# The high and low halves of the activations as one 512-column operand, in a split-precision transformer block on one core

## The reference, cut to what matters

```
for i in range(DEPTH):                                  # 2 layers
    sh1, sc1, g1, sh2, sc2, g2 = _ada(c, ada_w[i], ada_b[i])     # silu(c) @ ada_w + ada_b
    hx = _modulate(_rmsnorm(x, norm1_g[i]), sh1, sc1)
    yx = _mla(...)  if layer 0 else  _fourier_mix(hx, fno_w[j])  # both end in a 2048 x 2048 product
    x = x + g1 * yx
    x = x + g2 * _conv_ffn(_modulate(_rmsnorm(x, norm2_g[i]), sh2, sc2), ...)
return _rmsnorm(x, final_norm_g)

def _conv_ffn(h, w_up, conv_w, conv_b, w_down):         # D_FF = 5632
    u = _dwconv3(h @ w_up, conv_w, conv_b)              # 2048 -> 11264, then 3 taps along the tokens
    val, gate = jnp.split(u, 2, axis=-1)
    return (val * silu(gate)) @ w_down                  # 5632 -> 2048
```

## Time and profile before

| | |
|---|---|
| median of 3 runs | 2375.63 us (2371.57 to 2377.6) |
| the profiled execution's own time: first to last instruction | 2380.2 us |
| PE busy, its weight loads busy | 2240.8 us, 2151.0 us |
| DVE busy | 1778.1 us |
| ACT busy | 1116.4 us |
| the two square stages | about 535 to 632 and 1490 to 1588 us |
| up, layer 0: main part, second part | about 656 to 1021, 1223 to 1366 us |
| down, layer 0: main part, second part | about 1030 to 1213, 1366 to 1434 us |
| up, layer 1: main part (with ada steps to about 1800), second part | about 1610 to 1977, 2162 to 2300 us |
| down, layer 1: main part, second part | about 1977 to 2162, 2300 to 2366 us |

### The profile page before, as it was taken

How to read it: one execution, slowest core, us unless ns; L and a number is a source line. 1 busy time by engine, 2 the same in 40 slices (tenths; PEclk the granted TensorE clock), 3 DMA queues, 4 the chain that set the end, 5 groups by cost and what they waited for, 6 DMA issues and landing times.

```text
span 2380.2 us, 47926 instructions
## 1 busy us (share of the span) xinstructions
PE 2240.8 (94%) x17414; PEld 2151.0 (90%) x17414; DVE 1778.1 (75%) x2221; ACT 1116.4 (47%) x1441; POOL 178.9 (8%) x152
## 2 busy tenths in 40 slices
PE   5788888889899999999999999989999999999997
PEld 3268777779899999999999998989999999999997
DVE  4989677759888888878868886988886664445665
ACT  5742344433356666633335534336666663334542
POOL 0013100004300000000000040430000000000013
PEclk9989899989899999999989999989999999999999
DMA  8957434439677787779978781877775555555553
GB/s 304 339 184 278 153 133 141 129 104 328 237 259 271 271 273 276 271 279 371 370 257 272 278 261 49 304 261 257 273 247 184 186 183 170 185 185 180 183 184 124
DMA packets 149967, 546.90 MB, mean 230 GB/s; under 512 B 17040, under 2 KB 17552, under 8 KB 149648
## 3 DMA queue, kind: packets, MB, share of 16 engines
q1 hardware_dynamic: 149904, 546.04, 66.2%
HBM read 543.88 MB, written 2.10 MB: 229 GB/s over the span
## 4 chain that ended last, share of the span: by engine, by line
PE 81%; DVE 10%; issue 5%; ACT 2%; POOL 1%; DMA 1%; DVEq 0%; SPq 0%; ACTq 0%; POOLq 0%
PE bank L1133 24%; PE bank L1134 23%; PE bank L1135 23%; DVE w_lo L686 2%; PE bank L1163 2%; DVE acc L711 2%; PE bank L1139 1%; PE bank L1141 1%; PE bank L1140 1%; DVE w_lo L742 1%; PE bank L1316 1%; PE bank L1186 1%; PE bank L1195 1%; DMA x<-xT 1%; ACT w_hi L456 0%
## 5 line engine op out<-in xcount | busy, mean ns | idle before, releaser
L456 ACT CAST w_hi<-raw 128x1024 fp32r<-128x1024 f32 x638 | 665.3, 1048 | 644.1 <-PE bank L1135 596.9
L1133 PE MATMUL bank<-h_hi,w_hi 128*128 128x256 f32 x3216 | 920.3, 286 | 23.8 <-DVE w_lo L686 18.8
L686 DVE TENSOR_TENSOR w_lo<-raw,w_hi 128x1024 fp32r<-128x1024 f32 x642 | 780.7, 1228 | 187.9 <-ACT w_hi L456 187.8
L1134 PE MATMUL bank<-h_lo,w_hi 128*128 128x256 f32 x3216 | 917.3, 285 | 0.0
L1135 PE MATMUL bank<-h_hi,w_lo 128*128 128x256 f32 x3216 | 917.0, 285 | 0.0
L1133 PEld LDWEIGHTS bank<-h_hi,w_hi 128*128 128x128 f32 x3216 | 625.3, 194 | 28.2 <-issue 25.4
L1134 PEld LDWEIGHTS bank<-h_lo,w_hi 128*128 128x128 f32 x3216 | 625.4, 194 | 0.0
L1135 PEld LDWEIGHTS bank<-h_hi,w_lo 128*128 128x128 f32 x3216 | 624.9, 194 | 0.0
L711 DVE SCALAR_TENSOR_TENSOR acc<-ada,silu_c,acc 128x1024 f32<-128x1024 f32 x320 | 427.1, 1379 | 12.2 <-issue 9.4
L1133 PE MATMUL bank<-a_hi,w_hi 128*128 128x256 f32 x1408 | 395.9, 281 | 1.7 <-DVE a_lo L690 1.7
L1134 PE MATMUL bank<-a_lo,w_hi 128*128 128x256 f32 x1408 | 395.3, 281 | 0.0
(11 more groups left out here) (185 smaller groups left out, 2435.6 us busy)
## 6 DMA issues: line engine op xcount, KB each, us to landing
raw<-weights SPq DMA_DIRECT2D x642, 512.0 KB, 4.5
ada<-ada_late SPq DMA_DIRECT2D x320, 512.0 KB, 4.9
early<-ada_early SPq DMA_DIRECT2D x64, 512.0 KB, 5.4
ctx_s<-ctxT SPq DMA_DIRECT2D x1, 2048.0 KB, 7.8
x<-xT SPq DMA_DIRECT2D x1, 2048.0 KB, 12.2
outT<-h_pre SPq DMA_DIRECT2D x4, 512.0 KB, 2.7
dft_s<-dft SPq DMA_DIRECT2D x1, 768.0 KB, 5.6
conv_s<-conv SPq DMA_DIRECT2D x2, 176.0 KB, 3.7
```

The costliest lines, as they stand in the source:

```text
L456: act.copy(w_hi[:, slot, :], raw[:, slot, :]).then_inc(hi_done, 1)
L686: dve.tensor_tensor(w_lo[:, slot, :], raw[:, slot, :], w_hi[:, slot, :].bitcast(f32), ALU.subtract)\
L1133: pe.matmul(out, wh, hi_part, start=first, stop=False)
L1134: pe.matmul(out, wh, lo_part, start=False, stop=False)
```

## The change

The high and the low part of each activation tensor become one tensor with the part as second index (`h_hl`, `a_hl`, `f_hl`), so that one matmul can stream both: w_hi meets 512 columns (256 high, 256 low) and fills a whole bank, and w_lo then meets the 256 high columns and accumulates into the bank's first half. The bank's two halves have to be added afterwards. In `residual` a second multiply-add out of the second half follows the first, and waits for it. In the up stages ACT copies the second half into `part` and DVE adds the first half to it into `up_s`; this frees the bank. All three taps then read `up_s`, and the split that came after the taps comes between that addition and the taps. Silu now waits for `conv_done`, which the right tap raises.

```diff
-            mm = product(bank[4 + t][:, 0:SEQ], (c0 + e) % RING, k % 8, hh[:, k, :], hl[:, k, :], ...)
+            mm = halves(bank[4 + t], (c0 + e) % RING, k % 8, src[:, :, k, :], k == 0, k == KT - 1)
...
+            def halves(bank_, slot, u, pair, first, last):
+
+                cols = slice(u * UNIT, (u + 1) * UNIT)
+                pe.matmul(bank_[:, :], w_hi[:, slot, cols], pair, start=first, stop=False)
+                return pe.matmul(bank_[:, 0:SEQ], w_lo[:, slot, cols], pair[:, 0, :], start=False, stop=last)
...
 (ACT, in pair)
                     for g in range(2):
                         act.wait_ge(chunk_used, c + 2 * g + 2)
+                        act.copy(part[:, g, :], bank[(T0 + 2 * s + g) % 4][:, SEQ:2 * SEQ]).then_inc(part_done, 1)
+                        split(c + 6 + g, c0 + 2 + g)
                         taps = conv_s[:, bass.ds(2 * f + g, 1), :]
-                        act.activation(cv[:, s, g, :], bank[(T0 + 2 * s + g) % 4][:, 0:SEQ], ACT.Identity,
+                        act.wait_ge(tile_taken, T + g + 1)
+                        act.activation(cv[:, s, g, :], up_s[:, g, :], ACT.Identity,
                                        bias=taps[:, :, 3], scale=taps[:, :, 1]).then_inc(mid_done, 1)
-                        split(c + 6 + g, c0 + 2 + g)
-                    act.wait_ge(tile_taken, T + 2)
+                    act.wait_ge(conv_done, 2 * Pn + 2)
                     act.activation(cv[:, s, 1, :], cv[:, s, 1, :], ACT.Silu).then_inc(silu_done, 1)
...
 (DVE, residual)
-                dve.scalar_tensor_tensor(xm, bank[4 + e][:, 0:SEQ], g, xm, ALU.mult, ALU.add).then_inc(y_free, 1)
+                dve.scalar_tensor_tensor(xm, bank[4 + e][:, 0:SEQ], g, xm, ALU.mult, ALU.add).then_inc(y_half, 1)
+                dve.wait_ge(y_half, n_half)
+                dve.scalar_tensor_tensor(xm, bank[4 + e][:, SEQ:2 * SEQ], g, xm, ALU.mult, ALU.add).then_inc(y_free, 1)
...
 (DVE, in pair)
+                        dve.wait_ge(part_done, 2 * Pn + g + 1)
+                        dve.tensor_tensor(u, b[:, 0:SEQ], part[:, g, :], ALU.add).then_inc(tile_taken, 1)
+                        split(c + 6 + g, (c0 + 2 + g) % RING)
                         dve.wait_ge(mid_done, 2 * Pn + g + 1)
-                        dve.scalar_tensor_tensor(v[:, 1:SEQ], b[:, 0:SEQ - 1], t[:, :, 0], v[:, 1:SEQ],
+                        dve.scalar_tensor_tensor(v[:, 1:SEQ], u[:, 0:SEQ - 1], t[:, :, 0], v[:, 1:SEQ],
                                                  ALU.mult, ALU.add).then_inc(left_done, 1)
                         dve.wait_ge(left_done, 2 * Pn + g + 1)
-                        dve.scalar_tensor_tensor(v[:, 0:SEQ - 1], b[:, 1:SEQ], t[:, :, 2], v[:, 0:SEQ - 1],
-                                                 ALU.mult, ALU.add).then_inc(tile_taken, 1)
-                        split(c + 6 + g, (c0 + 2 + g) % RING)
+                        dve.scalar_tensor_tensor(v[:, 0:SEQ - 1], u[:, 1:SEQ], t[:, :, 2], v[:, 0:SEQ - 1],
+                                                 ALU.mult, ALU.add).then_inc(conv_done, 1)
```

More of the change, by code:

```diff
@@ L167, in backbone @@
         cursor[0] = phase_at
-        a_hi = place("a_hi", [P, PARTS[0], SEQ], f32r)
-        a_lo = place("a_lo", [P, PARTS[0], SEQ], f32r)
+        a_hl = place("a_hl", [P, 2, PARTS[0], SEQ], f32r)
+        a_hi, a_lo = a_hl[:, 0, :, :], a_hl[:, 1, :, :]
         cv = place("cv", [P, 2, 2, SEQ])
         ga = at("ga", [P, SEQ], f32, rs_at + 12 * SEQ)
+        part = at("part", [P, 2, SEQ], f32, rs_at)
+        up_s = at("up_s", [P, 2, SEQ], f32, sqt_at)
         acc1 = place("acc1", [P, D])
@@ L945, in _, with residual @@
             clear_accs(B_WO)
-            def residual(m, e, gate, *after):
+            def residual(m, e, gate, n_half, *after):
                 dve.wait_ge(*after)
@@ L986, in normed, with ffn @@
                         between(m)
-            def ffn(c0, T0, P0, layer):
+            def ffn(c0, T0, P0, Y0, layer):
                 dve.wait_ge(conv_in, 16 * (layer + 1))
@@ L1077, in _ @@
             dve.wait_ge(mod_done, MODS_EARLY + 1)
-            square(C_WO, B_WO, G1)
+            square(C_WO, B_WO, G1, Y_WO)
             dve.wait_ge(scl_done, 3)
@@ L1110, in _ @@
                     clear_accs(B_FNO)
-            square(C_FNO, B_FNO, 6 + G1)
+            square(C_FNO, B_FNO, 6 + G1, Y_FNO)
             def scale_l1f():
@@ L1119, in _ @@
             clear_accs(B_UP1)
[L1120 removed]
+            ffn(C_FFN1, T_UP1, FT, Y_FFN1, 1)
             norm(7, NRM_OUT)
@@ L1338, in _, with square @@
             ada_sum(1)
-            def square(c0, Y0, hh, hl):
+            def square(c0, Y0, src):
                 with pe.Fori(0, KT // 2) as i:
@@ L1361, in up @@
                         for g in range(2):
-                            mm = product(bank[(T0 + g) % 4][:, 0:SEQ], (c0 + 2 * g + k // 8) % RING, k % 8,
-                                         h_hi[:, k, :], h_lo[:, k, :], k == 0, k == KT - 1)
+                            mm = halves(bank[(T0 + g) % 4], (c0 + 2 * g + k // 8) % RING, k % 8, h_hl[:, :, k, :],
+                                        k == 0, k == KT - 1)
                             if k % 8 == 7 and g == 0:
@@ L1372, in up @@
                             pe.wait_ge(lo_done, c0 + 8 * i + e + 1)
-                        mm = product(bank[(T0 + g) % 4][:, 0:SEQ], (c0 + e) % RING, k % 8, h_hi[:, k, :],
-                                     h_lo[:, k, :], k == 0, k == KT - 1)
+                        mm = halves(bank[(T0 + g) % 4], (c0 + e) % RING, k % 8, h_hl[:, :, k, :], k == 0, k == KT - 1)
                         if k % 8 == 7:
@@ L1392, in ffn @@
                                 pe.wait_ge(a_ready, P0 + k + 8)
-                            mm = product(bank[4 + t][:, 0:SEQ], (c1 + e) % RING, k % 8, a_hi[:, k, :], a_lo[:, k, :],
-                                         k == 0, k == PARTS[0] - 1)
+                            mm = halves(bank[4 + t], (c1 + e) % RING, k % 8, a_hl[:, :, k, :], k == 0, k == PARTS[0] - 1)
                             if k % 8 == 7:
@@ L1411, in ffn @@
                             pe.wait_ge(a_ready, P0 + PARTS[0] + k + 1)
-                        mm = product(bank[4 + t % 2][:, 0:SEQ], c % RING, u % 8, a_hi[:, k, :], a_lo[:, k, :],
-                                     k == 0, k == PARTS[1] - 1)
+                        mm = halves(bank[4 + t % 2], c % RING, u % 8, a_hl[:, :, k, :], k == 0, k == PARTS[1] - 1)
                         if u % 8 == 7:
@@ L1419, in _ @@
             pe.wait_ge(o_taken, 1 + HEADS)
-            square(C_WO, Y_WO, h_hi, h_lo)
+            square(C_WO, Y_WO, h_hl)
             residual_sum(0)
@@ L1458, in _ @@
             pe.wait_ge(tile_taken, T_UP1)
-            square(C_FNO, Y_FNO, f_hi, f_lo)
+            square(C_FNO, Y_FNO, f_hl)
             residual_sum(2)
```

32 lines of the change are left out of this document (16 added, 16 removed).

## The result

| | before | after |
|---|---|---|
| median of 4 runs each, same chip | 2375.14 us (2371.57 to 2377.6) | 2405.71 us (2403.4 to 2410.12) |
| ratio, 95% interval | | 1.0121, 1.0101 to 1.0142 |
| span of the profiled execution | 2380.2 us | 2403.4 us |

The change makes the kernel slower by 30.6 us, 1.2%. The forecast was 2405, own range 2386 to 2428. The two profiled executions differ by 23.2 us only. Most of the other seven belong to the profile before, not to the change. Why the one before was slower is open.

The account below looks back on a forecast made before the run. PE was taken to bound up and down stages, DVE the squares and nearly the ada pairs; 18.6 + 2.5 + 26.2 - 17.4 = +29.9 on 2375.6 gave about 2405 us, own range 2386 to 2428, 8 in 10 2370 to 2440.

Parts of the forecast that it names:

- squares, 30 tiles: Square stages: DVE is the bound, and the second multiply-add lengthens each tile by 0.62 us, +18.6 us.
- ada pairs: Up pairs with ada steps: DVE becomes the bound, period from 11.52 to 11.98 us, +26.2 us.
- up, layer 1, without ada: Layer 1's 28 up pairs without ada: PE stays the bound and saves 0.36 us each, 10.1 us.
- down, layer 1: Layer 1's down stage: PE stays the bound, tiles go from 11.31 to 11.09 us, saving 4.8 us.
- down, layer 0: Layer 0's down stage: at most 4.8 us saved, half taken because of DMA and weight waits, 2.5 us.
- last residuals in the norm chains: Four norm chains: the last residual is exposed to the next norm, 4 x 0.62, +2.5 us.
- The exposed Silu: Ada up pairs: DVE waits for Silu, right tap to `ga` 1.07 us instead of 0.40, +0.67 us a pair.
- rival 1: Main-part up pairs: Silu's table load falls on the chain, +25 to +38 us, about 2435; chance 0.16.
- rival 2: PE's product: fixed part drops away, 0.320 us a product, net -15 us, about 2361; chance 0.09.
- rival 3: Ada up pairs: DVE's round fits under PE, below 11.16 us; total -18, about 2358; chance 0.06.

Follow-up runs that it names:

- Run 3: Changed kernel with both square stages as in the kernel before (three matmuls, one multiply-add): 2389.66 us, ratio 1.0046 to the kernel before.
- Run 4: Changed kernel with both additions ahead of the taps and the last split again before `ga`: 2389.08 us, ratio 1.005 to the kernel before.
- run 8: Changed kernel with squares as before, both additions first, and ada steps moved between `ga` and `a_lo`: 2354.16 us, ratio 0.9919 to the kernel before.
- run 11: Kernel of run 8 with ada steps first again in the last two pairs of layer 0's main up part: 2351.62 us, ratio 0.9894.
- run 1: Changed kernel with w_hi meeting the two halves in two 256-column matmuls again, additions kept: 2415.6 us, ratio 1.0154 to the kernel before.
- run 5: Changed kernel with the two halves of each tile side by side in memory: 2403.59 us, ratio 1.012 to the kernel before.
- run 7: Changed kernel once more, unaltered, for a second profile: one execution, 2412.89 us.
- run 6: Changed kernel with the up stages' ada steps on 256 of their 1024 columns: 2364.87 us, ratio 0.9952 to the kernel before.
- run 10: Kernel of run 8 with three 256-column matmuls for each product: 2386.21 us, ratio 1.003 to the kernel before.

## Why the prediction was right, and where its terms were off

The direction, the cause and the stages were right: PE's saving counts only where PE was and stays the bound, and DVE pays for two extra operations in all other stages. Term by term, from the two profiled executions:

| term | predicted | measured in the profile after |
|---|---|---|
| squares, 30 tiles | +18.6 (0.62 each) | +15.3 (0.51 each) |
| ada pairs | +26.2 (57 x 0.46) | +20.0 (31 x 0.32 + 12 x 0.39 + 16 x 0.34) |
| up, layer 1, without ada | -10.1 | -9.4 (16 x 0.43 + 12 x 0.21) |
| down, layer 1 | -4.8 | +0.9 (main part 0.0, second part +0.9, first to last `residual`) |
| down, layer 0 | -2.5 | -0.2 (main part -2.1, second part +1.9, first to last `residual`) |
| last residuals in the norm chains | +2.5 | +0.5 in the last of the four (last `residual` to the end, 14.16 to 14.69); the others not measured by themselves |
| sum | +29.9 | +27.1, so -3.9 is left to the span's 23.2 |

What is left lies where stages meet. The largest piece is from the last `ga` of layer 0's main up part to the first `residual` of its down stage, 20.3 us before and 16.6 after.

- **Squares.** The mechanism holds: DVE without a gap, PE idle in it. The term was mis-sized: I took the 0.62 us between left and right tap for the distance of two dependent multiply-adds, and here it is 0.50 (why the two differ was not tested). Run 3 shows that the stage costs what its tiles cost.
- **Ada pairs.** The term of 11.98 us came out at 11.84. The exposed Silu is 0.97 us from right tap to `ga`, not 1.07; an addition costs 0.335, not 0.35; the gap at the loop's branch is 0.27 (900.34 to 900.96 in place of 0.35), not 0.37. Together these are 0.10 + 0.03 + 0.05 a pair, a little more than the 0.14 to be explained. PE shows 0.37 us of idle time a pair, not the 0.8 predicted. That Silu is exposed, and that the gaps in DVE's list are handshakes which are no room for new work, was the step that decided. Run 4 shows it from the other side: with Silu partly covered again the kernel is 17 us faster by the ratios. Runs 8 and 11 cover the wait for the cast too and leave the squares alone, and come out below the old time.
- **Table load (rival 1).** It stays under the work of DVE. It starts before the right tap (886.54) does and ends at 887.01, just before Silu starts, so it is covered with next to nothing to spare:

```profile
885.73 1.28 ACT L629 ACT_TABLE_LOAD   x1
887.06 0.42 ACT L629 ACTIVATE cv<-cv 128x256 f32<-128x256 f32 x1
```

- **PE's product (rival 2).** 22.18 / 64 = 0.3466 us in the pairs without ada, predicted 0.349; never near 0.33. The Trainium skill's 2.5 ns for the fixed part of an isolated matmul ("TensorE: Matmul & The Clock Gate", section "Back-to-back issue gap"), by which a product would take an estimated 0.325 us, disagrees with the trace. The fixed part of this product is 27 to 33 ns for two matmuls (0.3466 or 0.3533 less 0.320).
- **DVE under PE (rival 3).** Excluded by run 1: 11.83 us with the old matmuls, 11.84 with the new.
- **Down, layer 1.** This step failed in the profiled execution. I predicted 11.09 a tile, with DVE and ACT nearly free; PE is gapless as I said, but at 0.3533 a product and not 0.347. No trace with the merged product has a down tile of 11.09: of the 20 main down stages in ten such traces 6 run at 11.165 and 14 at 11.31. The layout does not explain it (run 5); see below.
- **Second down parts, both layers.** The sum has no term for their start. The last `a_lo` now comes later after PE's last product, PE waits 4.0 and 2.0 us for it, and with the clock that fell behind it the parts take 1.9 and 0.9 us more, where a gain was predicted.
- **Down, layer 0.** The gain was halved for the DMA's sake. The main part shows no such limit: PE is gapless (22.32 of 22.32) with the DMA share at 0.97.
- **Range.** By its own terms (-11 and -6) its lower end is 2388, not 2386.

That the medians' difference, 30.6, meets the sum of 29.9 is partly luck: two costs were priced too high by 9.5 us and the gain too high by 8.7, and these two errors cancel. The terms above rest on one execution of each kernel, and the one before was longer than its timed runs, so they cannot be held against the 30.6 more closely than some 7 us.

## What to carry to other kernels

Before moving work off the busiest engine, take each stage's period and ask who sets it, then work out the other engine's own round with its handshakes counted as full, not as slack: here DVE, busy for 84% of the ada pairs, had room for 0.7 us a pair and was given 1.0 (a round of 11.84 for one of 10.80 to 10.84). Savings on one engine and costs on another do not add (-30 and +36 made +31), since the saving is lost wherever the cost makes the other engine the bound. And when the new bound is an in-order list with waits in it, look for work that can stand in those waits: the same two additions, with a split put back over Silu, the ada steps put where DVE waited for ACT's cast and the squares left alone, gave 0.9894 in place of 1.0121.

## What the runs showed of the hardware that was not expected

The new product, 512 and then 256 columns, each with its weight load, doesn't have one price. With PE gapless at full clock, 32 of them take 11.09, 11.165 or 11.31 us (0.3466, 0.3489 or 0.3533 each). One of these holds through a whole stage: 11.09 or 11.31 in the up stages, 11.165 or 11.31 in the down stages. Which one is not fixed by the program. Rows of DVE in the first execution of the changed kernel, two residuals of layer 0's down stage and two `ga` of layer 1's up stage, two rounds apart:

```profile
1102.53 0.48 DVE L958 SCALAR_TENSOR_TENSOR x<-bank,mod,x 128x256 f32 x1 [0.63 <-PE bank L1151]
1124.85 0.48 DVE L958 SCALAR_TENSOR_TENSOR x<-bank,mod,x 128x256 f32 x1 [0.63 <-PE bank L1151]
...
1900.56 0.42 DVE L1016 TENSOR_TENSOR ga<-cv 128x256 f32<-128x256 f32 x1 [0.48 <-ACT cv L629]
1922.76 0.43 DVE L1016 TENSOR_TENSOR ga<-cv 128x256 f32<-128x256 f32 x1 [0.48 <-ACT cv L629]
```

And in the second (run 7):

```profile
1103.14 0.48 DVE L958 SCALAR_TENSOR_TENSOR x<-bank,mod,x 128x256 f32 x1 [0.67 <-PE bank L1151]
1125.76 0.48 DVE L958 SCALAR_TENSOR_TENSOR x<-bank,mod,x 128x256 f32 x1 [0.66 <-PE bank L1151]
...
1894.92 0.42 DVE L1016 TENSOR_TENSOR ga<-cv 128x256 f32<-128x256 f32 x1 [0.48 <-ACT cv L629]
1917.53 0.42 DVE L1016 TENSOR_TENSOR ga<-cv 128x256 f32<-128x256 f32 x1 [0.48 <-ACT cv L629]
```

22.32 against 22.62 us in the first stage, 22.20 against 22.61 in the second. From the first to the last row of each stage that is 2.1 + 3.3 = 5.4 of the 7.7 us between the two spans, at a granted clock of 1.00 in all four windows and with no wait to show for it. So the profile of one execution can be 8 us beside another of the same kernel. Whether the execution or the chip decides is not separated by these two, which may be of different chips. For the execution speaks the spread on one chip: six executions of run 6 lie within 18.9 us and six of run 11 within 17.3, while fifteen of the kernel before lie within 10.2 and twelve of run 10, which has the old matmuls, within 8.9. The old form, three matmuls of 256 columns, took 0.3600 us in every up stage that PE paced and 0.3533 in nearly all down tiles.

What picks the rate stays open. The distance of the halves in memory is excluded (run 5 shows 11.09 and 11.31 as well). The load of DVE does not settle it either (run 6, 11.31 in all pairs with ada steps, with little work on DVE; run 8, 11.09 in all, with much). That the rates come from how weight loads and matmuls fall against each other on PE is a guess that no run here tests.
